# TensorE's order in a step of a two-branch mixer: nine products in the first burst, the last pieces ahead of the probabilities' turn

## What is computed

```python
h = rms_norm(x, g_pre_mix)
proj = h @ w_in
o_a = gated_delta_rule(q, k, v, g, beta)            # 4 heads of 128, in chunks
o_b = sliding_window_sink_attention(qb, kb, vb, attn_sinks)   # 8 heads of 64
mix = jnp.concatenate([o_a, o_b], axis=-1) @ w_out  # the output projection
x = x + rms_norm(mix, g_post_mix)
h = rms_norm(x, g_pre_ffn)                          # input of the channel sub-layer
```

## Time and profile before

| | us |
|---|---|
| median of 3 runs | 1318.95 |
| the three runs | 1317.91, 1318.95, 1320.73 |
| the profiled execution | 1318.86 |
| its span, first to last instruction | 1316.6 |
| TensorE busy | 1260.2 (96%) |
| VectorE busy | 697.7 (53%) |
| ScalarE busy | 411.3 (31%) |
| GpSimd busy | 151.1 (11%) |
| mean granted clock of TensorE | 0.986 of 2.4 GHz |

### The profile page before, as it was taken

One profiled execution on the slowest core, in us unless ns is written; L12 is line 12 of the kernel. 1 busy time (PEld: TensorE's weight loads), 2 busy tenths in 40 slices (PEclk: granted clock), 3 DMA queues, 4 the chain that ended last, 5 costly groups with the idle time before them and its releaser, 6 DMA issues.

```text
span 1316.6 us, 17348 instructions
## 1 busy us (share of the span) xinstructions
PE 1260.2 (96%) x6360; PEld 1065.5 (81%) x6360; DVE 697.7 (53%) x1068; ACT 411.3 (31%) x754; POOL 151.1 (11%) x184
## 2 busy tenths in 40 slices
PE   6999999996999999879999999999999999999997
PEld 5888888886888888758888888888888888888875
DVE  6332445557777677445554545353635353545366
ACT  5121334645444444243312121213131313131322
POOL 1221001203322222122000000000000000000005
PEclk9999999997999999979999999999999999999999
DMA  8321323553233332042101010111111111110033
GB/s 275 125 72 53 95 88 101 164 178 114 88 92 108 107 107 60 33 144 83 64 32 64 32 64 32 64 33 63 35 61 42 53 49 47 55 41 32 32 128 128
DMA packets 90762, 106.52 MB, mean 81 GB/s; under 512 B 17471, under 2 KB 75615, under 8 KB 90719
## 3 DMA queue, kind: packets, MB, share of 16 engines
q1 hardware_dynamic: 90719, 105.96, 24.8%
HBM read 82.84 MB, written 23.10 MB: 80 GB/s over the span
## 4 chain that ended last, share of the span: by engine, by line
PE 52%; POOL 1%; DVE 1%; issue 1%; ACT 0%; POOLq 0%
PE f_ps_up L2296 12%; PE f_ps_up L2295 12%; PE f_ps_up L2297 12%; PE sums L2306 5%; PE sums L2308 5%; PE sums L2307 5%; POOL stage L2015 1%; DVE split L2220 1%; POOL f_conv L2015 0%; POOL f_stat L2279 0%; DVE f_w_lo L2154 0%; ACT f_w_hi L2086 0%; POOLq L1920 0%; DVE f_conv L2233 0%; DVE h_t L2213 0%
## 5 line engine op out<-in xcount | busy, mean ns | idle before, releaser
L2295 PE MATMUL f_ps_up<-split,f_w_hi 128*128 128x512 f32 x704 | 274.9, 390 | 3.0 <-DVE split L2220 3.0
L2296 PE MATMUL f_ps_up<-split,f_w_hi 128*128 128x512 f32 x704 | 274.6, 390 | 0.0
L2297 PE MATMUL f_ps_up<-split,f_w_lo 128*128 128x512 f32 x704 | 274.6, 390 | 0.0
L2159 DVE SCALAR_TENSOR_TENSOR f_conv<-f_ps_up,f_taps,f_conv 128x1023 f32<-128x1023 f32 x88 | 112.8, 1282 | 274.5 <-ACT f_conv L2090 269.0
L2295 PEld LDWEIGHTS f_ps_up<-split,f_w_hi 128*128 128x128 f32 x704 | 132.5, 188 | 31.5 <-DVE f_w_lo L2154 2.1
L2297 PEld LDWEIGHTS f_ps_up<-split,f_w_lo 128*128 128x128 f32 x704 | 132.6, 188 | 27.7
L2296 PEld LDWEIGHTS f_ps_up<-split,f_w_hi 128*128 128x128 f32 x704 | 132.6, 188 | 27.3
L2090 ACT ACTIVATE f_conv<-f_ps_up,f_taps 128x1024 f32<-128x1024 f32 x44 | 53.1, 1208 | 324.9 <-PE f_ps_up L2297 324.9
L2171 DVE TENSOR_TENSOR h_t<-sums,h_t 128x512 f32<-128x512 f32 x168 | 111.0, 685 | 39.8 <-PE sums L2308 39.7
L2306 PE MATMUL sums<-f_w_hi,f_y_hi 128*128 128x512 f32 x320 | 124.6, 389 | 0.0
L2307 PE MATMUL sums<-f_w_lo,f_y_hi 128*128 128x512 f32 x320 | 124.5, 389 | 0.0
(11 more groups left out here) (293 smaller groups left out, 2064.7 us busy)
## 6 DMA issues: line engine op xcount, KB each, us to landing
stage<-in_w_up SPq DMA_DIRECT2D x22, 1024.0 KB, 5.1
stage<-in_w_down SPq DMA_DIRECT2D x11, 1024.0 KB, 4.8
x_tile<-in_x SPq DMA_DIRECT2D x12, 512.0 KB, 4.3
stage<-in_w_in SPq DMA_DIRECT2D x6, 1024.0 KB, 6.7
qkv<-conv SPq DMA_DIRECT2D x11, 512.0 KB, 3.6
rows<-p_row SPq DMA_DIRECT2D x8, 644.0 KB, 3.2
stage<-rows SPq DMA_DIRECT2D x8, 644.0 KB, 4.2
res<-x_tile SPq DMA_DIRECT2D x8, 512.0 KB, 3.0
```

The source lines that it names most:

```text
L2159: op = dve.scalar_tensor_tensor(conv[:, q, k:S], ps_up[:, q % 2, 0:S - k], taps[:, bass.ds(ct + (FTAPS - 1 - k) * 2 * FT, 1)], conv[:, q, ...
L2295: pe.matmul(bank, hi, h_hi[:, k, cols], start=(k == 0), stop=False)
L2296: pe.matmul(bank, hi, h_lo[:, k, cols], start=False, stop=False)
L2297: op = pe.matmul(bank, lo, h_hi[:, k, cols], start=False, stop=(k == KD - 1))
```

## The change

Only the order of TensorE's queue in the mix stage's steps changes. The first burst of the output projection takes a third k, three products more, ahead of `a_inv` at level 6; the second burst has these three fewer. In half 1 the last four k stand together, twelve products, ahead of `c_trp(t + 1, 1)`; before, six of them stood behind it and six behind `c_pv(t + 1, 1)`. No instruction is added or taken away, and the other engines' queues stay as they are.

```diff
                 B(a_vtr, par)
                 B(a_off, 6, a)
-                D_(d_mm, 0, [0, 1])
+                D_(d_mm, 0, [0, 1, 2])
                 B(a_inv, 6)
...
                 B(b_o2)
-                D_(d_mm, 0, [2, 3, 4, 5, 6, 7])
+                D_(d_mm, 0, [3, 4, 5, 6, 7])
                 A(c_scores, odd, 1)
                 D_(d_mm, 1, [0, 1, 2, 3])
                 if e:
                     d_tr2(t - 2, t)
+                D_(d_mm, 1, [4, 5, 6, 7])
                 A(c_trp, 1)
-                D_(d_mm, 1, [4, 5])
                 if n:
                     a_ktr(t + 2, par)
                     a_norms(t + 2)
                 A(c_pv, odd, 1)
-                D_(d_mm, 1, [6, 7])
```

## The result

The changed kernel takes 1323.4 us (median of 7 runs, 1320.97 to 1327.12) against 1318.95; the ratio of its runs to those of before is 1.0031, 95% interval 1.0016 to 1.0045. It is slower by 2.1 to 5.9 us. The forecast was 1320.2, its range ended at 1323.0. A second measurement on another chip, further down, gave 1.0017 (1.0003 to 1.0031). Over all 19 runs of the changed kernel and 90 of the kernel before that were taken with the first three series of experiments the means are 1322.52 and 1319.26, 3.3 us apart. The mean granted clock is 0.9815 in the changed kernel's runs and 0.9847 in those of before.

The account below looks back on a forecast made before the run. TensorE was taken to bound the mix steps; +1.13 in step 1, +0.42 in steps 2 to 5 and -0.33 in step 6 gave +1.2 us, plus or minus 0.7, so 1320.2 us, range 1316.3 to 1323.0.

Parts of the forecast that it names:

- What bounds it, first part: TensorE bounds the mix steps; three more products fill L1701's wait for VectorE's mask, gaining 0.69 us in steps 1 to 6.
- Second part, the old wait: Turn of the probabilities (L1779): its wait for ScalarE's exponentials goes, 4.1 us in steps 2 to 5, 0.44 in step 6.
- First new wait: TensorE waits for ScalarE's a_square at a_norms (L1615), 0.98 us in steps 1 to 5; step 6 loses 0.90 at values product.
- Second new wait: At L1713, heads of steps 2 to 6, TensorE waits 0.94 us for the delayed chain through ScalarE, VectorE and GpSimd.
- Rival (a): The second new wait at L1713 does not arise, only a_norms waits: 1315.5 us, faster; chance 0.12.
- Rival (b): The chain to L1713 is longer, +0.45 per step from five hand-overs longer by 0.09 each: 1322.5 us; chance 0.18.
- Rival (c), the clock: New holes drop TensorE's granted clock to 0.50, losing 2.5 us in each of five steps: 1332.7 us; chance 0.04.

Follow-up runs that it names:

- the late power: Changed kernel with GpSimd's power of the queries' norm (a_rq) one place later, behind d_rstd: 0.9993 and, on another chip, 1.0001 of before.
- work added: Four needless products per step ahead of the sums of squares, steps 1 to 5: 1.0021 of before on the changed kernel, 0.9987 with a_rq also behind d_rstd.
- six products at the end: Changed kernel with its last six products (half 1, k 6 and 7) put back behind the product with the values: 1.0026 of before.
- the second part alone: Kernel before with only half 1 changed, twelve products ahead of the turn of the probabilities, first burst still six: 1.0043 of before.
- the first part alone: Kernel before with only the bursts changed, first nine products, second fifteen, half 1 as before: 0.9994 of before.
- the two with early squares: Changed kernel with ScalarE's a_square ahead of the exponentials: 0.9992 of before; with a_rq also behind d_rstd: 0.9977.
- the two with products in between: Changed kernel with half 1's k 6 and 7 between the keys' turn and the sums of squares: 0.9966 of before; with a_rq also behind d_rstd: 0.9952.

## Why the prediction was wrong

Slower by 0.31% was measured; the forecast was 1.2 us slower, inside "no change", and the range ended 0.4 us too low. By the prediction's own steps:

- **What bounds it, first part.** Right. The wait of L1701 is gone, and the experiment with this part alone shows 0.69 a step moving to the turn.
- **Second part, the old wait.** Right: the turn waits in step 0 alone.
- **First new wait.** Right: 0.77 printed in steps 1 to 5, by starts 1.80 or 1.81 from turn to sums, where 1.86 was forecast; step 6 has 0.68 at L1787.
- **Second new wait.** Right where the clock held. From the turn to L1713 it is 9.17, 9.27 and 9.00 us at the heads of steps 2, 4 and 6; the forecast took 9.14. TensorE unhindered takes 8.31 (the late power's heads), where the forecast had 8.20, so the wait is 0.7 to 1.0 instead of 0.94.
- **Rival (a)** fell: the wait is there. **Rival (b)** fell too. It would have explained the time, and it ended near it (1322.5), but the chain is not longer.
- **Rival (c), the clock.** This is the step that failed: the sum took the granted clock to be 1.00 in steps 2 to 6 and put its loss at nothing, because one row of before showed holes without a fall. The rival stood at a chance of 0.04. At the heads of steps 3 and 5 the clock is at half for about 3.4 us. From the turn to L1713 it then takes 9.78 and 9.90 us, 0.7 more than the 9.15 of the other heads. A fall takes 1.5 us, and 0.8 of it comes out of the second wait. My price of 2.5 for each of five was wrong as well: I took a stretch that was cold throughout, set nothing off against the wait behind it, and had it happen every time. With two falls a run the sum is 1.2 + 1.4 = 2.6 us; the 19 runs give 3.3 with a standard error of 0.5, and the first series alone 2.1 to 5.9. So about 0.7 us is left. The table shows where 0.3 of it lies: steps 2 to 6 without falls (work added) are 1.3 us longer than before's, where the forecast's terms give 1.0. The other 0.4 is within the scatter. For the late power the terms were further off: between the two kernels with work added it wins 3.6 us, where 4.6 were expected.

Why I took (c) for unlikely: step 4 before had holes of 0.7 and 1.0 us at a clock of 1.00. But each of these stood directly behind a burst of the output projection's products or just ahead of one. The new hole has turns, sums of one column and products of 64 columns around it, and nothing of the projection until the next step's first burst, 15 us on. This is an argument and not shown: in the kernel with six products at the end a burst starts 1.8 us behind the hole's end, and the clock falls all the same. The section "A second HAM failure mode: psum-queue depth-cycling" of the Trainium skill's TensorE: Matmul & The Clock Gate, cited in the prediction as speaking against the change, tells of a kernel whose frequent short idle times between groups of products made the clock swing. I let one row of another arrangement outweigh it. The trace agrees with it here at 14 of the 30 heads behind the new hole, and at none of before's five.

Over all profiles taken: the six of kernels with an idle time ahead of the sums of squares (the changed kernel twice, the second part alone, the late power twice, the six products at the end) have falls at 14 of 30 heads. The eight without it (before, the first part alone, the two with added products, the two with early squares, the two with products in between) have none at 40. That the falls at these heads need the idle time ahead of the sums is shown by filling it and by removing it. Why it does so at about every second head and not at each is open; which heads differs from profile to profile.

## What to carry to other kernels

Filler work is worth what it covers: twelve products ahead of a wait that six all but covered (0.3 us is left of it in the order with products in between) uncovered two waits behind it, one of them a step later and three engines on. Follow the chain from the moved work through every in-order queue until it comes back to the bound engine. And do not price a new idle time of TensorE by one from another place: up to 1.7 us ahead of the turn and up to 1.3 us at L1713 left the clock alone, and 0.8 to 1.0 us ahead of the sums cost it at about every second head, with and without large products close behind. Needless products put into it cost nothing and kept the clock. To see an effect of 1 or 2 us, compare the same steps of two profiles, from head to head, and not whole times alone.

## What the hardware showed that I had not expected

- The granted clock fell to half for about 3.4 us behind an idle time of 0.8 to 1.0 us (printed) among small products, in 14 of 30 cases, and it did so also while large products were being issued (462.58 in the kernel with six products at the end).
- Executions of one kernel differ in this as well: the runs of before spread over 8 us, from a mean clock of 0.989 to one of 0.981, in part with the stretch behind step 0's 7.4 us wait, where the two profiles shown differ by 1.4 us. The later stages vary as well (the 787.2 to 790.8 us above), and in 530 to 565 us, the last step and what follows, the granted clock lies between 0.90 and 1.00, in before too (0.93). That is more than most changes here are worth, and the whole times of single profiles cannot decide them.
